# A feed-forward's down product: pairs two to four of two slabs as seven half-width products, with weight sums made on GpSimd

## The reference, cut to what matters

```python
def conv_ffn(h, w_up, conv_w, conv_b, w_down):
    u = h @ w_up                       # 1024 -> 2 * 2816
    c = u.shape[-1]
    u = lax.conv_general_dilated(      # three taps along the tokens, each channel by itself
        u, conv_w[:, None, :].astype(u.dtype), window_strides=(1,),
        padding=[(CONV_WIDTH - 1, 0)],
        dimension_numbers=("NWC", "WIO", "NWC"),
        feature_group_count=c) + conv_b
    a, gate = jnp.split(u, 2, axis=-1)
    return (jax.nn.silu(gate) * a) @ w_down    # 2816 -> 1024, added to x by the caller
```

## Time and profile before

| | |
|---|---|
| median of 3 runs | 3203.96 us (3202.7 to 3204.17) |
| span of the profiled execution | 3201.8 us |
| outside that span, against the median | 2.2 us |
| TensorE busy | 3186.1 us, 16,214 matmuls |
| VectorE, ScalarE, GpSimd busy | 1969.6, 1271.3, 404.6 us |

### The profile page before, as it was taken

How to read it: one execution, slowest core, us unless ns; L and a number is a source line. 1 busy time by engine, 2 the same in 40 slices (tenths; PEclk the granted TensorE clock), 3 DMA queues, 4 the chain that set the end, 5 groups by cost and what they waited for, 6 DMA issues and landing times.

```text
span 3201.8 us, 44978 instructions
## 1 busy us (share of the span) xinstructions
PE 3186.1 (100%) x16214; PEld 2672.4 (83%) x16214; DVE 1969.6 (62%) x2804; ACT 1271.3 (40%) x1734; POOL 404.6 (13%) x356
## 2 busy tenths in 40 slices
PE   9999999999999999999999999999999999999998
PEld 7788888889998788888889998768888888888887
DVE  8455567585557455557585555666665744585656
ACT  4433333334453433343334453254332523553423
POOL 2100000124221100000124221051000101320001
PEclk9999999999999999999999999999999999999999
DMA  7146324423323156324423322203222322122222
GB/s 267 67 167 206 126 94 167 140 92 106 106 99 106 55 169 208 121 98 166 142 87 106 106 99 83 86 21 112 99 99 93 105 99 92 47 85 100 92 99 79
DMA packets 100037, 359.24 MB, mean 112 GB/s; under 512 B 11056, under 2 KB 13360, under 8 KB 99760
## 3 DMA queue, kind: packets, MB, share of 16 engines
q1 hardware_dynamic: 98960, 354.08, 32.3%
q0 software_dynamic: 928, 3.17, 0.3%
HBM read 355.11 MB, written 2.10 MB: 112 GB/s over the span
## 4 chain that ended last, share of the span: by engine, by line
PE 94%; DVE 2%; POOLq 1%; issue 1%; ACT 1%; DVEq 1%; DMA 0%; ACTq 0%; SPq 0%; POOL 0%
PE pb L687 21%; PE pb L688 21%; PE pb L689 21%; PE pb L1002 6%; PE pb L719 2%; PE pb L720 2%; PE pb L723 2%; PE pb L759 2%; PE pb L757 2%; PE pb L758 2%; PE pb L1110 1%; PE pb L1485 1%; PE pb L1486 1%; PE pb L1487 1%; PE pb L978 1%
## 5 line engine op out<-in xcount | busy, mean ns | idle before, releaser
L1557 ACT ACTIVATE hi<-raw 128x1024 fp32r<-128x1024 f32 x500 | 524.8, 1056 | 850.0 <-PE pb L689 543.5
L2181 DVE TENSOR_TENSOR lo<-raw,hi 128x1024 fp32r<-128x1024 f32 (+1 forms) x500 | 617.6, 1241 | 330.1 <-ACT hi L1557 304.3
L687 PE MATMUL pb<-yH,hi 128*128 128x512 f32 (+1 forms) x1664 | 644.2, 387 | 0.0
L688 PE MATMUL pb<-yL,hi 128*128 128x512 f32 (+1 forms) x1664 | 644.0, 387 | 0.0
L689 PE MATMUL pb<-yH,lo 128*128 128x512 f32 (+1 forms) x1664 | 643.9, 387 | 0.0
L687 PE MATMUL pb<-hH,hi 128*128 128x512 f32 x1128 | 440.5, 391 | 0.0
L688 PE MATMUL pb<-hL,hi 128*128 128x512 f32 x1128 | 439.0, 389 | 0.0
L689 PE MATMUL pb<-hH,lo 128*128 128x512 f32 x1128 | 438.9, 389 | 0.0
L687 PEld LDWEIGHTS pb<-yH,hi 128*128 128x128 f32 x1664 | 312.5, 188 | 63.6
L689 PEld LDWEIGHTS pb<-yH,lo 128*128 128x128 f32 x1664 | 312.4, 188 | 63.5
L688 PEld LDWEIGHTS pb<-yL,hi 128*128 128x128 f32 x1664 | 312.5, 188 | 63.4
(11 more groups left out here) (486 smaller groups left out, 5237.5 us busy)
## 6 DMA issues: line engine op xcount, KB each, us to landing
raw<-stream SPq DMA_DIRECT2D x648, 512.0 KB, 3.3
yF<-first SPq DMA_DIRECT2D x8, 512.0 KB, 12.0
act<-first SPq DMA_DIRECT2D x8, 512.0 KB, 16.5
x<-xT SPq DMA_DIRECT2D x4, 512.0 KB, 7.6
outT<-act SPq DMA_DIRECT2D x7, 256.0 KB, 2.2
act<-crow POOLq DMA_DIRECT2D x2, 512.0 KB, 5.6
tab<-decay SPq DMA_DIRECT2D x1, 1024.0 KB, 7.8
scr<-ws POOLq DMA_DIRECT2D x2, 256.0 KB, 3.1
```

What stands on the lines that cost most here:

```text
L687: pe.matmul(out, whi, ahi, start=first, stop=False)
L688: pe.matmul(out, whi, alo, start=False, stop=False)
L1557: act.activation(hi[:, s], raw[:, s], ACT.Copy).then_inc(hi_ready, 1)
L2181: dve.tensor_tensor(lo[:, s, 0:width], raw[:, s, 0:width], hi[:, s, 0:width].bitcast(F32), ALU.subtract).then_inc(lo_ready, 1)
```

## The change

In slabs 0 and 1 of both layers the down part is done otherwise (`fast_down`); slab 2 stays. Output tiles 0 and 1 are still taken plainly, block by block, two together. Tiles 2 to 7 form three groups of two tiles. In a group the slab's middle activations are split in two by block parity and in two by token half, and the weights in two by tile and in two by block parity (the host reorders the blocks for this). Seven products of 4 x 3 matmuls of 256 columns stand in place of 2 x 24 matmuls of 512 columns. Their operands are:

- sums of the middle activations, t1 to t4, of 256 columns per pair of blocks: on GpSimd for the first three pairs (`middle_sums`), on VectorE for the last; rounded by ScalarE (`middle_hi`), rest by VectorE (`middle_lo`);
- sums of weights, four operations of 512 columns per group on GpSimd (`down_sums`), of which the second overwrites half of the group's second tile, so that this tile's own tick has to wait for it (`s1_ready`). All three groups' sums stand in GpSimd's queue behind a wait for the slab's last `y_ready`;
- VectorE adds six pieces per group to `x` from the banks (`x_adds`), three of which release TensorE's next product (`x_part`).

SP's loop over the stream is cut at these slabs: the tiles that take the slots of a group wait for that group's weight sums. A new 128 x 6 x 512 buffer holds sums, `rows` and `zT` swap places, and the scratch for transfers issued by GpSimd is set to 4096 bytes.

```diff
+FAST_DOWN, DOWN_GROUPS = (0, 1), (1, 2, 3)
...
+        d_sum = lambda q: act3[:, 4:7] if q else ext[:, 0:3]
+        d_sumL = lambda q: halved[:, 4:7] if q else extR[:, 0:3]
+        d_sumH = lambda q: tabR[:, 1:4] if q else extR[:, 3:6]
+        d_even = act3[:, 7]
...
+            loaded = early
+            for layer in range(LAYERS):
+                for j in FAST_DOWN:
+                    n = d_tile(layer, j) + RING
+                    into_ring_from(loaded, n)
+                    for g in range(FAST_GROUPS):
+                        if g in DOWN_GROUPS:
+                            sp.wait_ge(w_sums, d_at(layer, j, g) + 1)
+                        into_ring(n + 2 * g)
+                        into_ring(n + 2 * g + 1)
+                    loaded = n + KT
+            into_ring_from(loaded, TILES)
...
+            def down_sums(layer, j, g):
+                e, at = d_sum(g % 2), d_at(layer, j, g)
+                four_sums(d_tile(layer, j) + 2 * g, [e[:, i] for i in range(3)],
+                          5 * (at - 1 if g == 3 else at if g == 1 else at - 2))
+            def four_sums(n, sums, unread):
+                s0, s1 = n % RING, n % RING + 1
                 a11, a12, a21, a22 = raw[:, s0, 0:S], raw[:, s0, S:2 * S], raw[:, s1, 0:S], raw[:, s1, S:2 * S]
-                e2, e3, e4 = (act3[:, e_at(q, i)] for i in (2, 3, 4))
+                e2, e3, e4 = sums
                 pool.wait_ge(landed[s0], 16 * (n // RING + 1))
                 pool.wait_ge(landed[s1], 16 * (n // RING + 1))
-                if fast_at(l, j, g) >= 2:
-                    pool.wait_ge(p_full, 5 * (fast_at(l, j, g) - 1))
+                if unread is not None:
+                    pool.wait_ge(p_full, unread)
                 pool.tensor_tensor(e3, a11, a21, ALU.subtract)
                 pool.drain()
                 pool.tensor_tensor(a21, a21, a22, ALU.add)
...
                 pool.drain()
                 pool.tensor_tensor(e4, a12, e2, ALU.subtract)
                 pool.drain().then_inc(w_sums, 1)
...
+            def middle_sums(layer):
+                for j in FAST_DOWN:
+                    made = d_product(layer, j)
+                    for k in range(3):
+                        b1, b2 = d_even, A[:, 2]
+                        t1, t2, t3, t4 = (d_raw(i, k) for i in (1, 2, 3, 4))
+                        pool.wait_ge(product, made + 2 * k + 1)
+                        pool.tensor_tensor(t1, b1[:, TH[1]], b1[:, TH[0]], ALU.subtract)
+                        pool.wait_ge(product, made + 2 * k + 2)
+                        pool.tensor_tensor(t3, b2[:, TH[1]], b1[:, TH[1]], ALU.subtract)
+                        pool.drain()
+                        pool.tensor_tensor(t2, t3, b1[:, TH[0]], ALU.add)
+                        pool.drain()
+                        pool.tensor_tensor(t4, b2[:, TH[0]], t2, ALU.subtract)
+                        pool.drain().then_inc(m_sums, 1)
+                    pool.wait_ge(y_ready, d_middle(layer, j) + KT)
+                    for g in DOWN_GROUPS:
+                        down_sums(layer, j, g)
...
+            def fast_down(layer, j, y0):
+                for s in range(2):
+                    pe.wait_ge(lo_ready, tiles.next())
+                    pe.wait_ge(bank_free, banks.next())
+                for m in range(KT):
+                    w = slice((m % 2 * 4 + m // 2) * P, (m % 2 * 4 + m // 2 + 1) * P)
+                    pe.wait_ge(y_ready, y0 + m + 1)
+                    for s in range(2):
+                        ins = three(pb[:, s], hi[:, s, w], lo[:, s, w], midH[:, m], midL[:, m], m == 0, m == KT - 1)
+                        if m == KT - 1:
+                            ins.then_inc(tile_done, 1)
+                for g in DOWN_GROUPS:
+                    down_group(layer, j, g)
...
+                upper, other_sum, one_sum, lower_sum = (pb[:, b, 0:256] for b in (2 * q, 2 * q + 1, 4 + 2 * q, 5 + 2 * q))
+                s0, s1 = 2 * q, 2 * q + 1
+                own = lambda s, k: [w[:, s, k * S:(k + 1) * S] for w in (hi, lo)]
+                summed_w = lambda i: (d_sumH(q)[:, i - 2], d_sumL(q)[:, i - 2])
+                middle = lambda k, t: (midH[:, k::2, TH[t]], midL[:, k::2, TH[t]])
+                token = lambda i: (d_tokH(i), d_tokL(i))
...
+                pe.wait_ge(lo_ready, tiles.next())
+                pe.wait_ge(bank_free, banks.next(2))
+                product_of(one_sum, own(s0, 0), middle(0, 0)).then_inc(p_full, 1)
+                product_of(upper, own(s0, 1), middle(1, 0)).then_inc(tile_done, 1)
+                pe.wait_ge(lo_ready, tiles.next())
+                if g == DOWN_GROUPS[0]:
+                    pe.wait_ge(m_lo, tokens_made)
+                product_of(other_sum, own(s1, 0), token(1)).then_inc(p_full, 1)
+                product_of(lower_sum, own(s1, 1), token(4)).then_inc(tile_done, 1)
+                pe.wait_ge(e_lo, at + 1)
+                pe.wait_ge(x_part, added + 1)
+                product_of(one_sum, summed_w(2), token(2), False).then_inc(p_full, 1)
+                pe.wait_ge(x_part, added + 2)
+                product_of(other_sum, summed_w(4), middle(1, 1), False).then_inc(p_full, 1)
+                pe.wait_ge(x_part, added + 3)
+                product_of(one_sum, summed_w(3), token(3), False).then_inc(p_full, 1)
...
+                    if j in FAST_DOWN:
+                        fast_down(layer, j, y_k.value())
+                    elif last:
                         first_T(midH, midL, (y_ready, y_k.value()), n)
...
+            def down_hi(layer, j, g, part):
+                s = 2 * (g % 2) + part
+                act.wait_ge(landed[s], land[s].next(16))
+                if part:
+                    act.wait_ge(s1_ready, d_at(layer, j, g) + 1)
+                act.wait_ge(tile_done, split.next())
+                act.activation(hi[:, s], raw[:, s], ACT.Copy).then_inc(hi_ready, 1)
+            def down_sum_hi(layer, j, g):
+                act.wait_ge(w_sums, d_at(layer, j, g) + 1)
+                act.activation(d_sumH(g % 2), d_sum(g % 2), ACT.Copy).then_inc(e_hi, 1)
+            def middle_hi(k):
+                act.activation(d_tokens[0][:, :, k], flat_hF[:, 4:8, k], ACT.Copy).then_inc(m_hi, 1)
...
+                        if fast and i % 4 == 1 and m:
+                            act.wait_ge(m_sums, 3 * slab + m // 2)
+                            middle_hi(m // 2 - 1)
                     gate(n - 1)
                     first += n
-                    if j < len(SLABS) - 1:
-                        tiles_T(8, lambda i, s: None, uses_st=False)
+                    if fast:
+                        act.wait_ge(m_last, slab + 1)
+                        middle_hi(3)
+                        down_hi(layer, j, 1, 1)
+                        down_sum_hi(layer, j, 1)
+                        for g in (2, 3):
+                            down_hi(layer, j, g, 0)
+                            down_hi(layer, j, g, 1)
+                            down_sum_hi(layer, j, g)
+                        done.next(KT)
+                        for s in (1, 2, 3):
+                            tick(s)
...
+            def down_sum_lo(layer, j, g):
+                dve.wait_ge(e_hi, d_at(layer, j, g) + 1)
+                dve.tensor_tensor(d_sumL(g % 2), d_sum(g % 2), d_sumH(g % 2).bitcast(F32), ALU.subtract).then_inc(e_lo, 1)
+            def middle_lo(layer, j, k):
+                dve.wait_ge(m_hi, 4 * d_slab(layer, j) + k + 1)
+                dve.tensor_tensor(d_tokens[1][:, :, k], flat_hF[:, 4:8, k], d_tokens[0][:, :, k].bitcast(F32), ALU.subtract
+                                  ).then_inc(m_lo, 1)
...
+                def one_of():
+                    dve.wait_ge(p_full, p + 1)
+                    dve.tensor_tensor(x0[:, TH[0]], X, x0[:, TH[0]], ALU.add).then_inc(x_part, 1)
...
+            def fast_down(layer, j):
+                one, other, two, lower, upper, last = x_adds(layer, j, 1)
+                middle_lo(layer, j, 3)
+                down_lo(layer, j, 1, 1)
+                for k in range(2):
+                    drained.next()
+                    dve.wait_ge(tile_done, done.next())
+                    dve.tensor_tensor(x[:, k], pb[:, k], x[:, k], ALU.add).then_inc(bank_free, 1)
+                one()
+                down_sum_lo(layer, j, 1)
+                other()
+                down_lo(layer, j, 2, 0)
+                lower()
+                two()
+                down_lo(layer, j, 2, 1)
+                upper()
+                last()
...
+                        if fast and m % 2 == 0 and m:
+                            dve.wait_ge(m_sums, 3 * slab + m // 2)
+                        dve.tensor_tensor(product_at(m), A[:, s], A[:, s + 1], ALU.mult)
...
+                        if fast and i % 4 == 2 and m >= 3:
+                            middle_lo(layer, j, m // 2 - 1)
...
-                    if j < len(SLABS) - 1:
-                        add_to_x(8)
+                    if fast:
```

(60 more changed lines are left out.)

101 lines of the change are left out of this document (78 added, 23 removed).

## The result

The changed kernel takes 3217.97 us (median of 4 runs, 3217.85 to 3219.29) against 3203.8 (4 runs, 3202.7 to 3204.17): 14.2 us more, a ratio of 1.0046 with a 95% interval of 1.0032 to 1.0060. The profiled execution's span is 3216.2 us against 3201.8, 14.4 more. Ratios and intervals leave out the few launches that ran far longer than all others (one of 10,250 us in experiment 2, one of 4530 us in experiment 4).

What follows compares the result with a forecast made beforehand. TensorE, busy 3186.1 of 3201.8 us, was taken to bound the kernel. Two first slabs at +5.4 and two second slabs at +2.6 made +16.0 us, from 3203.96 to 3220; range 3197 to 3227.

Steps and rivals of the forecast that it cites:

- the main case: Whole kernel: waits in the four changed slabs add 16.0 us, to 3220; own range 3212 to 3224, chance 0.42.
- TensorE's saving: Down part: 84 matmuls of 256 columns replace 48 of 512, gaining 0.80 us per group, 9.6 us over 12 groups.
- The turns: Behind the last `y_ready`: VectorE and GpSimd alternate instructions with two SBUF operands; VectorE's four small sums end 5.4 us later.
- The last `y_ready`: From the down part's start: 6.6 us in second slabs, about 9.4 in first; TensorE needs it at 9.5.
- the lower bound: First slabs: if VectorE's waits for ScalarE absorb the added work, the shift is nothing; bounds 0 and 2.8 us.
- The wait for slot 3: Group 1: TensorE waits for the second tile's tick, 3.1 us in second slabs and 5.9 in first.
- The second and third wait: Group 1: TensorE waits 1.5 us for the sums' rest, then 0.3 us at the product needing `two`.
- signs of being wrong: Profile after: GpSimd starting later than said, arrears at tile 15 gone, or a step in the granted clock.
- No wait, faster: Rival: the engines happen to miss each other, so TensorE never waits in down parts: -9.6 us, 3194; chance 0.20.
- half of it: Rival: t1 and t3 pass before GpSimd wakes, 3.5 us per slab, no arrears: +4.4 us, 3208; chance 0.22.
- the clock falls as well: Rival: idle TensorE drops to 1.2 GHz, costing 1 to 2.5 us per slab: 3224 to 3230; chance 0.16.
- Edits at nothing: SP's split loops, adds to `x`, swapped buffers, reordered weights and smaller scratch cost nothing; scratch loss below 2 us if any.

Runs made afterwards that it cites:

- experiment 2: Changed kernel, but GpSimd's weight sums of group 2 wait for the rest of group 1's sums: 3215.57 us, ratio 1.0039.
- experiment 4: Changed kernel with the weight sums left out: GpSimd adds only 16 columns and fills the sums with zeros: 3194.92 us, ratio 0.9973.
- with the clock kept: Changed kernel with small identity matmuls (13 in second slabs, 20 in first) ahead of TensorE's wait for the second tile: 3217.31 us, ratio 1.0042.
- Experiment 3: Changed kernel with tiles 2 and 3 also taken plainly, two fast groups left per slab: 3196.88 us, ratio 0.9981.
- The reordered version: Changed kernel with group 1's sums early, groups 2 and 3 behind group 1's rest, ScalarE's and VectorE's order changed: 3206.91 us, ratio 1.0010.

## Why the prediction was right, step by step

The forecast was +16.0 us and 3220; measured were +14.2 and 3217.97, inside the main case's own range of 3212 to 3224. By the slab lengths it is +15.4, and the earlier start of the stage hides 1.0 of it.

- **TensorE's saving**, 0.80 us per group. Right: 41.12 predicted and 41.11 measured for a slab without waits, 41.92 and 41.91 with two groups. Such a slab is 2.4 us shorter than before (43.52 - 41.11). By the Trainium skill's formula (TensorE: Matmul & The Clock Gate, section "Wait — 56ns, not 53.3ns?") the gain would be 3 x 1.19 = 3.6, an estimate; the measurement decides for 0.80.
- **The turns.** Right, and the core of it. Predicted was t4's end 5.3 to 5.4 us after the last `y_ready`; it came after 5.9 (2288.8 to 2294.7 in the timeline). GpSimd's sums of group 1 took 1.29 each: it never waited, since it was first at each turn. The price of the overlap was visible in the earlier trace rows before, in another stage. One reading of them was a little off: the differences there are 0.8 to 1.3 us and not each the whole of the other engine's instruction (1.22 and 1.28), and the turn that experiment 2 takes away is 1.1.
- **The last `y_ready`** at 6.6: measured 6.65 in the second slabs. In the first ones 9.4 was predicted, and it came at 8.1 and 8.5. The sum made of the earlier trace rows was too dear here by 1 us: VectorE's waits for ScalarE took up a part of the added work, as the lower bound allowed. Before, they were 2.5 and 2.3 us in the last 45 us of the first slabs' up parts; in the changed kernel there are none. The first slabs cost 4.6 and 5.4 instead of 5.4.
- **The wait for slot 3.** Predicted 3.1 and 5.9, four in all, 18.0 together; measured 16.8, as 3.4 and 3.3 in the second slabs and 4.8 and 5.2 in the first. The second slabs' is longer by the slower turns, the first slabs' shorter by the smaller arrears.
- **The second and third wait**, 1.5 and 0.3 per slab. This is the step that failed in form. The changed kernel has neither. I had set the fall of the clock apart as a rival when it belongs to the main case. A step in the granted clock was also one of the signs of being wrong, and it is there. The lower clock makes the matmuls behind the wait longer (21 in 4.57 us instead of 2.52, in the first slab's windows), and in that time the rest arrives. The two costs have one place and don't add: what the slab pays behind the first wait is the larger of them. For the second slab, idle 3.4, and 46.26 - 41.11 - 3.41 = 1.7 are left for the clock and waits; 1.8 was predicted for the waits alone. In the first slabs 2.2 and 2.6 are left. That is why the total hardly noticed, and it is luck that the two have nearly one size.
- **The rivals.** "No wait, faster" and "half of it" are refuted by the view of waits and by the strict turns. The mechanism of "the clock falls as well" is real in all four slabs, its price is not: with the clock kept the second slab moved by 0.2 us, the four slabs together by 2.0 and the median by 0.7, where the rival asked for 4 to 10. The Trainium skill's rule (TensorE: Matmul & The Clock Gate, section "HAM oscillation — how this bites in real kernels") that gaps throttle TensorE again holds in the granted clock here (0.51 behind a gap of 5.00 us).
- **Edits at nothing.** Experiment 3 contains SP's split loop, the reordered weights and the smaller scratch, and its four slabs lack nothing of the gain. These edits cost nothing there.

What stays open: the clock's own price is known only from one pair of profiled executions, 2.0 us in the four slabs, of which the medians show 0.7; and the difference in how early the stage begins (about 1 us either way between executions) is traced to the program's first 50 us, but why executions differ there isn't explained. A fix that keeps three fast groups and is faster than before was not found. The reordered version comes nearest, and its rest is VectorE's arrears in the first slabs.

## What to carry to other kernels

Before work that reads SBUF is moved to GpSimd, list what VectorE does with two SBUF operands in the same microseconds, and count them as one queue, one instruction of each in turn. Then ask how soon the result is needed: the same turns cost 16.8 us of waiting where TensorE wants the second tile 7 us after the last `y_ready`, and nothing where it wants it after 18. When a fast form of a product needs prepared operands, start it one group later, since here eight fast groups (3196.88) beat twelve (3217.97).

## What the runs showed of the hardware that was not expected

A stop of TensorE of 2.3 us (experiment 2, second slab) already brings the lower clock, some 0.5 us after the restart. The windows there, of experiment 2:

```profile
2431.24:2434.00 2.76, 2.76 (x15) 0.60 0.53 190
2434.00:2437.00 3.00, 3.00 (x22) 0.80 0.00 0
```

And the timeline of TensorE there:

```profile
2431.47 0.28 PE L1316 MATMUL pb<-hL,hi 128*128 128x256 f32 x1
2431.59 0.28 PE L1316 MATMUL pb<-hH,lo 128*128 128x256 f32 x1
...
2431.85 0.42 PE L1316 MATMUL pb<-hL,hi 128*128 128x256 f32 x1
2432.06 0.42 PE L1316 MATMUL pb<-hH,lo 128*128 128x256 f32 x1
```

The first starts behind the stop are 0.12 apart, at full clock, and from 2431.85 on 0.21. And a slow clock behind a wait need cost nothing, as in that second slab, 45.7 us with it and without it: if the next operand is late by as much, speeding TensorE up turns slow matmuls into a wait, and only the page's busy time changes.
